# Experts of a mixture layer: eight consecutive weight rows per partition, with the token columns written in the matching order

## The reference

```python
def hier_moe(h, w_grp, b_grp, w_exp, b_exp, w_gate, w_up, w_down):
    grp_logits = h @ w_grp + b_grp              # 4 groups
    exp_logits = h @ w_exp + b_exp              # 32 experts, 8 in each group
    ...                                         # best group, then its 2 best experts per token
    def expert_block(args):                     # xb: 128 tokens of one expert
        xb, e = args
        return (silu(xb @ w_gate[e]) * (xb @ w_up[e])) @ w_down[e]
    ...                                         # weighted sum of a token's two results
```

## Time and profile before

| what | value |
|---|---|
| median of 3 runs | 4604.64 us (4602.85 to 4605.74) |
| profiled execution | 4605.19 us |
| its span in the trace | 4603.4 us |
| mean granted clock of TensorE | 0.896 |
| TensorE busy | 3762.6 us (82% of the span) |
| DVE, ACT, POOL busy | 1256.8, 776.3, 617.4 us |
| DMA moved | 697.06 MB, mean 151 GB/s |

### The profile page before, as it was taken

How to read it: one execution, slowest core, us unless ns; L and a number is a source line. 1 busy time by engine, 2 the same in 40 slices (tenths; PEclk the granted TensorE clock), 3 DMA queues, 4 the chain that set the end, 5 groups by cost and what they waited for, 6 DMA issues and landing times. The chain is left out here.

```text
span 4603.4 us, 102874 instructions
## 1 busy us (share of the span) xinstructions
PE 3762.6 (82%) x45908; PEld 2388.3 (52%) x45908; DVE 1256.8 (27%) x2933; ACT 776.3 (17%) x1775; POOL 617.4 (13%) x792
## 2 busy tenths in 40 slices
PE   3499996799996449968888887879999739997787
PEld 1245644455553124547777776355555414564464
DVE  0114112211110161035555454531111120232153
ACT  0101001000000010034333332010000010231142
POOL 0000000111110010035444342001111100000000
PEclk8799997899998769979999998779999969858999
DMA  8621114699995442210000000279999733101100
GB/s 335 245 81 46 69 37 147 245 382 378 377 375 197 156 107 73 76 40 15 17 17 17 19 17 28 91 280 382 376 375 372 281 93 103 62 1 47 37 38 23
DMA packets 297354, 697.06 MB, mean 151 GB/s; under 512 B 26013, under 2 KB 49021, under 8 KB 296284
## 3 DMA queue, kind: packets, MB, share of 16 engines
q1 hardware_dynamic: 262780, 602.53, 36.2%
q0 software_dynamic: 26192, 73.25, 4.9%
q10 hardware_dynamic: 7952, 14.81, 0.8%
HBM read 636.40 MB, written 54.14 MB: 150 GB/s over the span
## 5 line engine op out<-in xcount | busy, mean ns | idle before, releaser
L847 PE MATMUL banks<-w_gate_up_ring,x_turned 128*32 128x256 f32 x12288 | 695.4, 382 | 68.2 <-DMA w_gate_up_ring<-in_moe_w_up_dram 66.9
L847 PEld LDWEIGHTS banks<-w_gate_up_ring,x_turned 128*32 128x32 f32 x12288 | 429.8, 110 | 307.5 <-issue 94.5
L865 PE MATMUL banks<-w_down_ring,hidden_turned 128*32 128x256 f32 x6144 | 344.8, 380 | 0.0
L923 DVE TENSOR_TENSOR hidden<-silu_gate,banks 128x128 f32<-128x128 f32 x192 | 55.3, 288 | 804.4 <-ACT silu_gate L903 790.0
L827 POOL DMA_DIRECT2D y_rows<-y_out_rows x256 | 140.9, 559 | 985.6 <-ACT y_out_rows L909 947.4
L865 PEld LDWEIGHTS banks<-w_down_ring,hidden_turned 128*32 128x32 f32 x6144 | 193.1, 110 | 128.6
L361 PE MATMUL banks<-const_cols,h_tokens 128*128 128x128 f32 x240 | 54.1, 404 | 223.2 <-DVE h_tokens L334 151.3
L1844 DVE TENSOR_TENSOR inverse_both_ways<-banks,inverse_both_ways 128x512 f32<-128x512 f32 (+1 forms) x240 | 152.2, 637 | 251.5 <-PE banks L1753 250.6
L815 POOL DMA_INDIRECT x_rows<-h_rows,cell_index x64 | 62.7, 979 | 867.5 <-POOLq L42 841.4
L449 PE MATMUL banks<-gmlp_weights,h_turned_gmlp 128*128 128x512 f32 x384 | 166.9, 598 | 13.0 <-DMA gmlp_weights<-in_ga_w_in_dram 13.0
L1742 PE MATMUL banks<-inverse_both_ways,l_quarters 64*64 64x64 f32 x3840 | 148.6, 222 | 34.5 <-POOL inverse_both_ways L1926 26.6
(11 more groups left out here) (446 smaller groups left out, 5530.5 us busy)
## 6 DMA issues: line engine op xcount, KB each, us to landing
w_gate_up_ring<-in_moe_w_gate_dram SPq DMA_DIRECT2D x68, 2048.0 KB, 10.7
w_gate_up_ring<-in_moe_w_up_dram SPq DMA_DIRECT2D x68, 2048.0 KB, 24.9
w_down_ring<-in_moe_w_down_dram SPq DMA_DIRECT2D x68, 2048.0 KB, 20.3
ada_ring<-in_ada_w_dram SPq DMA_DIRECT2D x12, 4096.0 KB, 25.0
y_rows<-y_out_rows POOLq DMA_DIRECT2D x256, 96.0 KB
gmlp_weights<-in_ga_w_in_dram SPq DMA_DIRECT2D x8, 2048.0 KB, 8.3
ab_weights<-in_ab_w_in_dram SPq DMA_DIRECT2D x6, 2048.0 KB, 8.8
gmlp_weights<-in_ga_w_out_dram SPq DMA_DIRECT2D x4, 2048.0 KB, 8.3
```

Of the source, the lines that this page charges most:

```text
L847: last = pe.matmul(ps[strip(j), GU + g, 0:2 * FQ].rearrange("p (a c) -> p a c", a=2), xT[:, e % 2, k, strip(g)], wgu[:, e % 2, :, k, j * F ...
L865: last = pe.matmul(ps[strip(j), Y + g // 2, (g % 2) * DQ:(g % 2 + 1) * DQ], hT[:, g, strip(k)], wd[:, e % 2, k, j * DQ:(j + 1) * DQ], star ...
```

## The change

The DRAM views of gate and up are read as `(p k)` in place of `(k p)`. Partition p now holds rows 8p to 8p + 7, which lie one after the other in DRAM, and so do its eight slices in the tile: 16 KB in one piece on both sides. Slice k of partition p is then row 8p + k. The router's weights are read in the same order. For the columns of the tokens to match, the MoE's tiles of `h` are written so that column 8c + k of the token lands at place 128k + c: the product of L331 goes to a separate tile (`product`, which is the tile `junk` of the squares), and the addition of the shift reads that tile in its own order and writes `h` with a step of 128 elements between successive values. From the second tile on, DVE waits for its own earlier addition before it refills `product`. The kept rows `h_rows`, the turned `hT` and the gathered rows then all have the new order without any other edit. The down weights, the results and the `norm_turn` calls without `keep` stay as they were.

```diff
--- before.py
+++ after.py
@@ -278,6 +278,7 @@
         spread = sb("spread_rows", [P, len(srcs), D])
         h = sb("h_tokens", [P, 2, D])
         junk = sb("squares", [P, D])
+        product = junk
         ss = sb("sum_squares", [P, n])
         rs = sb("rstd", [P, n])
         sems = held.enter_context(signals(nc, "spread_in squared rooted rstd_ready scaled h_ready turned moved_low moved_high dve_chain act_chain"))
@@ -328,10 +329,17 @@
                         if keep is not None:
                             dve.wait_ge(kept[j % 2], 16 * (j // 2))
                     g, s = place[name(gains[j])], shifts[j]
-                    op = dve.scalar_tensor_tensor(h[:, j % 2, :], core.x[:, t, :], rs[:, j:j + 1], spread[:, g, :], ALU.mult, ALU.mult)
+                    scaled_x = h[:, j % 2, :] if keep is None else product[:, :]
+                    if keep is not None and j:
+                        dve.wait_ge(h_ready, j)
+                    op = dve.scalar_tensor_tensor(scaled_x, core.x[:, t, :], rs[:, j:j + 1], spread[:, g, :], ALU.mult, ALU.mult)
                     if s is not None:
                         chain(op)
-                        op = dve.tensor_tensor(h[:, j % 2, :], h[:, j % 2, :], spread[:, place[name(s)], :], ALU.add)
+                        if keep is None:
+                            op = dve.tensor_tensor(h[:, j % 2, :], h[:, j % 2, :], spread[:, place[name(s)], :], ALU.add)
+                        else:
+                            op = dve.tensor_tensor(h[:, j % 2, :].rearrange("p (k c) -> p c k", k=KD), scaled_x[:, :].rearrange("p (c k) -> p c k", k=KD),
+                                                   spread[:, place[name(s)], :].rearrange("p (c k) -> p c k", k=KD), ALU.add)
                     op.then_inc(h_ready, 1)
                     if j >= 1:
                         evacuate(j - 1)
@@ -618,8 +626,8 @@
         index = sb("cell_index", [CAP, nb], I32)
         home = sb("row_of_choice", [P, 2, nt], U32)
         beyond = sb("blocks_beyond", [P, blocks_beyond(nt) + 1], I32)
-        gate_src = ins["moe_w_gate"][layer].rearrange("e (k p) f -> e p k f", p=P)
-        up_src = ins["moe_w_up"][layer].rearrange("e (k p) f -> e p k f", p=P)
+        gate_src = ins["moe_w_gate"][layer].rearrange("e (p k) f -> e p k f", p=P)
+        up_src = ins["moe_w_up"][layer].rearrange("e (p k) f -> e p k f", p=P)
         down_src = ins["moe_w_down"][layer].rearrange("e (k p) d -> e p k d", p=P)
         wr = sb("router_w", [P, KD, ROUTER])
         br = sb("router_b", [P, ROUTER])
@@ -630,8 +638,8 @@
         def loads(sp):
 
             with nc.allow_non_contiguous_dma(reason="router weights: rows of 4 and 32 columns"):
-                sp.dma_start(wr[:, :, 0:NG], ins["moe_w_grp"][layer].rearrange("(k p) n -> p k n", p=P)).then_inc(router_in, 16)
-                sp.dma_start(wr[:, :, NG:], ins["moe_w_exp"][layer].rearrange("(k p) n -> p k n", p=P)).then_inc(router_in, 16)
+                sp.dma_start(wr[:, :, 0:NG], ins["moe_w_grp"][layer].rearrange("(p k) n -> p k n", p=P)).then_inc(router_in, 16)
+                sp.dma_start(wr[:, :, NG:], ins["moe_w_exp"][layer].rearrange("(p k) n -> p k n", p=P)).then_inc(router_in, 16)
                 sp.dma_start(br[:, 0:NG], rows(ins["moe_b_grp"], layer * NG, NG)).then_inc(router_in, 16)
                 sp.dma_start(br[:, NG:], rows(ins["moe_b_exp"], layer * E, E)).then_inc(router_in, 16)
             for r in range(2):
```

## The result

| | before | after |
|---|---|---|
| median (lowest to highest) | 4604.64 us (4602.21 to 4610.01) | 4623.54 us (4618.15 to 4631.47) |
| profiled execution / its span | 4605.19 / 4603.4 us | 4622.78 / 4621.0 us |
| DMA packets | 297354 | 175498 |
| mean granted clock of TensorE | 0.896 | 0.894 |

What follows compares the result with a forecast made beforehand. DMA engines set the expert stages' pace, 19.0 us per expert against PE's 17.39. From 4605.2 us: -36 for faster loads, -1 passes beyond, +3 norm stages, giving 4571 us; own range 4550 to 4592, wide range 4540 to 4612.

Steps and rivals of the forecast that it cites:

- The joining of the runs: Gate and up loads: 1024 runs of 2 KB become 128 of 16 KB, packets falling from 297354 to about 175500.
- The rate of larger runs: Expert stages: gate and up load faster in 16 KB runs, 0.6 us per expert, near the 8.4 KB row's rate.
- the price put on 4 KB: Expert stages, lower end: one expert gains 0.1 us at the 4 KB row's 409 GB/s, against 405.
- the upper end: Expert stages: most gain per expert, 0.95 us, from 10.64 us for gate and up at 394 GB/s; -57 us in all.
- 60 x 0.6: Expert stages, both layers: 60 refilled experts gain 0.6 us each, -36 us, with ends at -6 and -57.
- the -1 of the passes beyond: Four passes beyond: a gate load alone is 0.35 us shorter at 434 GB/s than at 405, -1 us.
- the +3 of the norm stages: Norm stages, ten tiles: +0.6 us per slower addition, half of them exposed, +3 us, with ends 0 and +12.
- Rival (d): Small packets wait behind 16 KB ones: gather +3.1 us, hidden in `experts`, +12.6 over four passes beyond; chance 0.15 shared with (c).
- The strided addition: Norm stage, L334: writing with a 512-byte step takes between 1225 and 2367 ns, ten times.
- Rival (c): Weight loads: larger pitch slows them, at 363 GB/s +55 us, 4663 with the norm; chance 0.15 shared with (d).
- Rival (a): Weight loads: runs joined but rate hardly moves, or not joined; 4602 us, from 4592 to 4614; chance 0.18.
- That nobody waits for SP's own time: SP's time issuing an up load, blocked behind its full queue, should shrink, which nobody waits for; no size given.

Runs made afterwards that it cites:

- the stages of loads: Kernel before with stages of gate-weight loads put ahead, alone or beside small transfers; alone, loads moved 387 GB/s at 2 KB, 410 at 4 KB, 425 to 428 at 16 KB.
- the kernel before with the late loads: Kernel before, with SP issuing the first two experts' weights only once the kept copies have landed: 4618.82 us, ratio 1.0039.

## Why the prediction was wrong

- **The joining of the runs** held: 175498 packets for 175500, and SP's issue of an up load fell from a median of 7.60 us to 0.43.
- **The rate of larger runs** was right in direction and too small in size. From a window of 1.5 us I took 0.6 us per expert; the loads alone give 1.02. But the windows of 3 us for 2 KB rows, 405 and 406 GB/s, were the worse guide: over 35 us such loads move 387, while the 409 of the 90 us window for 4 KB held (410). It is not the 3 us as such, for in the steady stream such windows read 385 to 389. A single load of 2 MiB lasts 5.4 us at 387 GB/s, less than two of them, and the window's place decides: 1 us earlier (1772 to 1775) the 406 of the kernel before is 384. The step that looked like 1% is 6%, so the price put on 4 KB, 0.1 us per expert, should have been 0.6, and the size that gains was not seen. (From its own rows the upper end was 0.98 us, 10.64 - 9.66, and not 0.95; nothing hangs on that.)
- **The step that failed** is the one from the rate alone to the stage: "60 x 0.6". It let everything else in the stage stand at its old price. The small transfers did not stay there: a gather's price went from 1.8 to 3.1 us. The -36 us of the expert stages came out as -2 (+1.4 and -3.4), the -1 of the passes beyond as +13.7, and the +3 of the norm stages as +12.9. The dips of the rate, which the prediction saw as the distance between 394 and 377 GB/s, were the term to ask about, since the stages of loads show them while gathers or reads of a second queue are in flight, and the change makes the packets of one of the two queues eight times as large.
- **Rival (d)** was right in its mechanism and nearly in its size: +3.1 us for a gather and +12.6 for the four passes beyond, where the passes took +13.7 and the waits grew by 3.1 to 4.5, 3.9 on average. Its two errors were of place. It called the delay hidden in `experts`; from PE it is hidden (12.6 us of waiting now, 12.7 in the earlier trace rows), but the loads pay for it. And it looked at gathers only. The kept copies are 4 KB packets beside the same loads, and the prediction had named DVE's wait of 6.29 us for one of them itself: they take 4.3 us longer. Of the 12.9 us that the norm stages lost, the kernel without the stride shows 4.2 to be the stride's, and 8.7 are left for the copies; since the stride costs nothing beside 2 KB packets, those 4.2 too need the late copies.
- **The strided addition** lies inside its bounds, 1913 ns between 1225 and 2367; +3 us for both layers was taken, the kernel without the stride shows 1.8 and 2.4. The rule cited from the Trainium skill (Advanced Engine Details and Errata, section Memory Cachelines) is borne out in direction, with 0.69 us for 128x1024.
- **Rival (c)**, the pitch, is out: at the larger pitch loads of 2 KB pieces move the same 387 GB/s, and whole 16 KB ones 428. Rival (a) is out as a cause; that its time, 4602, lies nearer to the measured one is chance.
- That nobody waits for SP's own time holds where the loads are issued early. In the kernel before with the late loads DVE's idle time at the end of the stage grew from 7.96 to 23.77 us behind it.

## What to carry to other kernels

A packet size is chosen for all queues that are busy at once, not for one. Where small reads fly beside a stream of loads, try the stream cut at 4 KB: here this took most of the rate (410 of 428 GB/s) and delayed a gather by 0.8 us in place of 7, and the same kernel went from 0.4% slower to 0.5% faster. And when a change alters the packets of one queue, list every transfer of the other queues in the same stretches, look which of them somebody waits for, and price them again.

## What the runs showed of the hardware

- Loads from DRAM in runs of 2, 4, 8 and 16 KB: 387, 410, 423 and 428 GB/s over 35 us each, and no difference between runs that lie together and runs 128 rows apart at 2 KB.
- 96 reads of 4 KB beside such loads land after 6.5 to 6.8, 6.9 to 8.1, 8.2 to 8.8 and 10.4 to 11.0 us; beside 16 KB with two loads in flight in place of four, after 10.0 to 11.6.
- While a gather of another queue is in flight, the total rate falls to some 270 to 340 GB/s at any packet size, for 2 us beside 2 KB, 3 beside 4 KB and 4 to 6 beside 16 KB (windows of 1 us), at a DMA share near 1.0. Plain reads lower the mean rate too, writes do not. Why reads and not writes was not found. Nor was the difference between a gather's lost time at 16 KB in the stage of loads (1.56 us and its own 0.92) and in the kernel (3.12 by taking it away, 2.1 to 2.5 by adding one).
- An addition of 128x1024 float32 whose writes step by 512 bytes takes 1913 ns, a contiguous one 1225.
- The end of a stage can hang on the engine that only issues transfers: an up load of 1024 runs held SP for 7.6 us in the median and up to 11.0, one of 128 runs for 0.43 and at most 1.6.
